# State space stage: half of the input projection in quarters between the scan's first pairs, phases and sine tables during the other half

## The chip, the core and the metric

The kernel runs on one core of a Trainium2 chip. A core has five engines with queues of their own: TensorE (PE in the profile, with its weight loads as PEld), VectorE (DVE), ScalarE (ACT), GpSimd (POOL) and SyncE (SP), which here only issues DMAs. They wait for one another by semaphores. The metric is the time of one execution in device microseconds (us), lower is better.

## The reference

Two networks follow one another. The first mixes with a gated delta rule and attention, then with a convolution; the second has three mixers in turn (an HGRN, an mLSTM, and a state space mixer, "S5"), each followed by a feed-forward stage, on 256 tokens of 1024 channels. Everything is computed in float32. The change touches only the last mixer:

```python
def _s5_mixer(x, w_in, a_re, a_im, log_dt, b_re, b_im, c_re, c_im, d_skip, w_out):
    u = (x @ w_in).astype(f32)
    dt = jnp.exp(log_dt.astype(f32))[:, None]
    mag = jnp.exp(a_re * dt)
    abar_re = mag * jnp.cos(a_im * dt)
    abar_im = mag * jnp.sin(a_im * dt)
    ...
    def step(carry, ub):
        hr, hi = carry
        bu_re = jnp.einsum('blgc,gpc->blgp', ub, bbar_re)
        bu_im = jnp.einsum('blgc,gpc->blgp', ub, bbar_im)
        pr, pi, sr, si = lax.associative_scan(_s5_combine, (a_r, a_i, bu_re, bu_im), axis=1)
        ...
        y = jnp.einsum('blgp,gcp->blgc', sr, c_re) - jnp.einsum('blgp,gcp->blgc', si, c_im)
        return (sr[:, -1], si[:, -1]), y
    ...
    y = y + d_skip.astype(f32) * u
    y = jax.nn.gelu(y).astype(x.dtype)
    za, zb = jnp.split(y @ w_out, 2, axis=-1)
    return za * jax.nn.sigmoid(zb)
```

`abar` is a complex number; a state is turned by its angle and shrunk by `mag` at every token.

## The kernel before

Activations lie with channels on the 128 partitions and the 256 tokens along the free axis (T = 256), in KC = 8 chunks. The program is a list of stages; each stage writes its part of every engine's queue, by hand and in program order, so the order of the code is the order of the queues. Weights come as slabs of 1 MB through a ring of five buffers that SyncE fills as they are freed. L216 is the helper that issues every matmul with weights. PSUM has eight banks: seven (BANKS) go round as jobs, and the eighth, `mod_bank`, is used by the first network's modulation.

The S5 mixer is two stages.

`S5In` projects the input: four slabs (`project_columns`), each two chunks of 128 channels and 16 products of 128x128 by 128x256, into a bank; ScalarE copies each bank to `u` (L3334). Beside it ScalarE and VectorE prepare coefficients in `columns`, 32 numbers a partition: `R_DT` (L3351, the angle in turns), `R_MAG` and `R_SIN` and `R_COS`, then with L3343 and a few others `R_CR` and `R_CI`; then VectorE scales the read-out matrices, loaded by DMA, in six operations over 1024 elements (L3379 to L3384) and two scalings (L3385, L3386). The last one raises `ready`.

`S5Scan` works through 32 tiles of 128 states, in 16 pairs. For a tile i:
- GpSimd makes the phase of every token (L3515 to L3517, three operations over 256 elements; two buffers, so tile i waits for the sines of tile i - 2). It waits for `ready` first.
- ScalarE makes a table of cosine and two sines (L3493 to L3499, five operations). There are six table buffers, so tile i waits until tile i - 6 has been turned back.
- TensorE projects the pair's input to states (L3468, `project`), VectorE multiplies it by the table (`turn`, L3527 and L3528), TensorE adds the terms up (L3450 and L3451, the "rotations"), VectorE scans in PSUM (`scan`, L3539 and L3540), multiplies by the table again (`turn_back`, L3550 and L3551), and TensorE reads out (L3482, `read_out`). Every fourth tile an output chunk is finished (L3573).

VectorE's order in pair m is scan(2m), scan(2m+1), turn(2m+2), turn(2m+3), perhaps a finish, turn_back(2m), turn_back(2m+1). TensorE's order in pair m is the rotations of 2m and 2m+1, the projection of pair m+1, the read-out of pair m-1. `project(m)` needs the copy of slab m // 4.

Of the kernel before, what the change touches and what calls it, by code (L numbers as in the profile page):

```python
# [21 lines left out]
P = 128  # L22
# [3277 lines left out]
class S5In(Stage):  # L3300


    def setup(self):
        k = self.k
        self.x_ready = k.h_ready
        self.slab0 = k.weights.reserve(4, False)
        self.u = k.area(S_U, KC, T)
        self.u_ready = k.counter("mixer_q").events(4)
        self.jobs = [k.job(e) for e in self.u_ready]
        self.loaded = k.counter("s5_matrices_loaded")  # L3310
        self.dt_ready = k.counter("s5_dt").event()
        self.prod_ready = k.counter("s5_products").events(2)
        self.exp_ready = k.counter("s5_exp").event()
        self.sin_ready = k.counter("s5_sin").event()
        self.ready = k.counter("decay_cumulated").event()

    def tensor(self, pe):
        project_columns(self.k, pe, (self.k.h,), self.x_ready, self.jobs)

    def scalar(self, act):  # L3320
        k, c = self.k, self.k.cols
        for e in self.x_ready:
            act.wait_ge(*e)
        act.dma_start(k.area(S_BC, 4096), k.s5_bc).then_inc(self.loaded.sem, 16)
        act.activation(c[:, R_DT, :], k.v("s5_log_dt", 0, S5_TILES), ACT.Exp).then_inc(self.dt_ready[0], 1)
        act.wait_ge(*self.prod_ready[0])
        act.activation(c[:, R_MAG, :], c[:, R_MAG, :], ACT.Exp).then_inc(self.exp_ready[0], 1)
        act.wait_ge(*self.prod_ready[1])

        act.activation(c[:, R_SIN, :], c[:, R_TH, :], ACT.Sin)  # L3330
        act.activation(c[:, R_COS, :], c[:, R_TH, :], ACT.Sin, scale=0.5).then_inc(self.sin_ready[0], 1)
        for j in range(4):
            act.wait_ge(*self.jobs[j].full)
            act.activation(self.u[:, 2 * j:2 * j + 2, :], pair(self.jobs[j]), ACT.Identity)\  # L3334
               .then_inc(self.u_ready[j][0], 1)

    def vector(self, dve):
        k, c, link = self.k, self.k.cols, self.k.dve.link
# [9 lines left out]
        tt(R_TH, aim, row(R_DT), mult)  # L3348
        reduce_angle(dve, link, row(R_TH), row(R_N), self.prod_ready[1])

        link(dve.tensor_scalar(row(R_DT), row(R_TH), 1.0 / TWO_PI, None, mult))  # L3351
        dve.wait_ge(*self.exp_ready)
        dve.wait_ge(*self.sin_ready)

# [18 lines left out]

        dve.wait_ge(self.loaded.sem, 16)
        out = k.area(S_BC + 2048, 2, S5_TILES, 32)
        t1, t2 = k.area(S_PH, S5_TILES, 32), k.area(S_T1, S5_TILES, 32)
        cr = row(R_CR).unsqueeze(2).broadcast_to([P, S5_TILES, 32])
        ci = row(R_CI).unsqueeze(2).broadcast_to([P, S5_TILES, 32])
        link(dve.tensor_tensor(t1, out[:, 0, :, :], ci, mult))  # L3379
# [20 lines left out]
class S5Scan(Stage):  # L3400
# [32 lines left out]
    def tensor(self, pe):  # L3433
        k = self.k
        b = k.area(S_BC, KC * 2, P)
        pe.wait_ge(self.src.loaded.sem, 16)
        pe.wait_ge(*self.src.ready)
        for bank in (*self.bu_banks, *self.g_banks, self.y_bank):
            begin(pe, bank)
        self.project(pe, b, 0)  # L3440
        for m in range(S5_PAIRS):
            for i in (2 * m, 2 * m + 1):
                bank = self.g_banks[i % 2].ap
                t1, t2 = self.turned[:, i % 2, 0:2, :], self.turned[:, i % 2, 2:4, :]
                pe.wait_ge(*self.turned_ready[i])
                if m >= 1:
                    pe.wait_ge(*self.scanned[i - 2])
                for part in range(2):
                    out = bank[:, part * T:(part + 1) * T]
                    pe.matmul(out, k.c("ident"), t1[:, part, :], start=True, stop=False)  # L3450
                    mm = pe.matmul(out, self.neg, t2[:, 1 - part, :], start=False, stop=True)  # L3451
                mm.then_inc(self.g_full[i][0], 1)
            if m + 1 < S5_PAIRS:
                self.project(pe, b, m + 1)
            if m >= 1:
                self.read_out(pe, m - 1)
        self.read_out(pe, S5_PAIRS - 1)
# [27 lines left out]

    def scalar(self, act):
        k = self.k
        for i in range(S5_TILES):
            table = self.table[:, i % S5_TABLES, :, :]
            act.wait_ge(*self.phase_ready[i])  # L3490
            if i >= S5_TABLES:
                act.wait_ge(*self.back_ready[i - S5_TABLES])
            act.activation(table[:, 1, :], self.phase[:, i % 2, 0, :], ACT.Sin, scale=TURN)  # L3493
            act.activation(table[:, 2, :], self.phase[:, i % 2, 0, :], ACT.Sin, scale=-TURN)
            act.activation(table[:, 0, :], self.phase[:, i % 2, 0, :], ACT.Sin, scale=0.5 * TURN)\
               .then_inc(self.sin_done[i][0], 1)
            act.wait_ge(*self.sin_done[i])
            k.act.link(act.activation(table[:, 0, :], table[:, 0, :], ACT.Square))
            act.activation(table[:, 0, :], table[:, 0, :], ACT.Identity, bias=k.eps[:, 2:3], scale=-2.0)\  # L3499
               .then_inc(self.table_ready[i][0], 1)  # L3500
# [4 lines left out]
    def gpsimd(self, pool):  # L3505

        k = self.k
        pool.wait_ge(*self.src.ready)
        for i in range(S5_TILES):
            if i >= 2:  # L3510

# [343 lines left out]
```

## Time and profile before

| | |
|---|---|
| three timed runs | 2686.16, 2687.28, 2688.93 us, median 2687.28 |
| the profiled execution | 2674.91 us, span 2673.1 us |
| busy in the span | PE 89%, PEld 80%, DVE 58%, ACT 40%, POOL 4% |
| input projection of S5, four slabs | 1802.18 to 1831.77 us |
| scan, first rotations to last read-out | 1835.84 to 1956.1 us |

The page gives busy shares for the whole span, the groups of instructions by line, and the chain of waits that ended last. The order of time gives for every piece its start, its length, the engine, the line, what it writes and reads, and in brackets how long the engine had been idle and who released it. The stage of the change is 154 us of the 2673, so the argument rests on its own stretch.

### The profile page before, as it was taken

How to read it: one execution, taken by the hardware profiler on the slowest of the kernel's cores; microseconds unless marked ns; L12 is line 12 of the kernel's file. 1: busy time of each engine (PE TensorE's matmuls, PEld its weight loads, DVE VectorE, ACT ScalarE, POOL GpSimd, SP SyncE). 2: the span in 40 equal slices, each digit the busy share in tenths (PEclk: the TensorE clock that was granted, in tenths of full speed). 3: DMA queues.
4: the chain of work that ended last, by engine and by line, in shares of the span. 5: the costliest groups of instructions: out<-in, count | busy, mean ns of one | idle time of the engine just before them, and what ended most of it. 6: DMA issues, size and time to landing. Idle time of an engine off the chain costs nothing.

```text
span 2673.1 us, 40276 instructions
## 1 busy us (share of the span) xinstructions
PE 2388.1 (89%) x17042; PEld 2151.2 (80%) x17042; DVE 1558.9 (58%) x2585; ACT 1067.4 (40%) x1682; POOL 111.3 (4%) x119
## 2 busy tenths in 40 slices
PE   6998998999889999589998879999998999757998
PEld 3665788998679989569997759997678998756998
DVE  3386456646846555556656446657946655664655
ACT  2424334443244345234444334434514335613443
POOL 0012000000000000000000000005600000000000
PEclk8999998999999999799998779999998999978999
DMA  7236353552135544014553115542034554301552
GB/s 294 111 142 259 136 181 135 189 190 79 64 142 187 187 158 164 14 48 176 189 188 111 64 47 190 190 158 79 1 111 163 186 188 152 117 1 49 203 190 80
DMA packets 50292, 368.27 MB, mean 138 GB/s; under 512 B 5568, under 2 KB 5696, under 8 KB 5824
## 3 DMA queue, kind: packets, MB, share of 16 engines
q1 hardware_dynamic: 49968, 363.59, 37.5%
q8 instruction: 135, 2.21, 0.3%
q10 hardware_dynamic: 144, 2.10, 0.2%
q14 instruction: 45, 0.37, 0.0%
HBM read 364.62 MB, written 1.05 MB: 137 GB/s over the span
## 4 chain that ended last, share of the span: by engine, by line
PE 79%; DVE 13%; ACT 5%; issue 2%; DMA 1%; SPq 0%; DVEq 0%; ACTq 0%
PE psum L216 63%; PE psum L2861 3%; DVE weight_parts L209 1%; PE psum L3450 1%; PE psum L3451 1%; DMA weight_ring<-stream_dram 1%; PE psum L2484 1%; PE psum L3187 1%; DVE work L949 1%; PE psum L398 1%; DVE work L2935 1%; DVE work L2936 1%; PE psum L1589 1%; PE psum L3468 1%; PE psum L543 1%
## 5 line engine op out<-in xcount | busy, mean ns | idle before, releaser
L216 PE MATMUL psum<-input_parts,weight_parts 128*128 128x256 f32 x8064 | 979.1, 284 | 57.0 <-DVE input_parts L957 27.3
L216 PEld LDWEIGHTS psum<-input_parts,weight_parts 128*128 128x128 f32 x8064 | 973.7, 192 | 64.8 <-issue 59.1
L209 DVE TENSOR_TENSOR weight_parts<-weight_ring,weight_parts 128x1024 fp32r<-128x1024 f32 x492 | 579.8, 1220 | 301.9 <-ACT weight_parts L193 300.9
L193 ACT ACTIVATE weight_parts<-weight_ring 128x1024 fp32r<-128x1024 f32 x492 | 492.9, 1052 | 198.1 <-PE psum L216 192.9
L216 PE MATMUL psum<-hidden_parts,weight_parts 128*128 128x256 f32 x3168 | 377.2, 281 | 0.0
L216 PE MATMUL psum<-work,weight_ring 128*128 128x256 f32 (+1 forms) x1376 | 354.7, 419 | 23.6 <-DVE work L2952 10.1
L216 PEld LDWEIGHTS psum<-hidden_parts,weight_parts 128*128 128x128 f32 x3168 | 374.6, 188 | 0.5
L216 PEld LDWEIGHTS psum<-work,weight_ring 128*128 128x128 f32 x1376 | 270.1, 198 | 103.6 <-issue 67.0
L1038 DVE TENSOR_TENSOR work<-work,psum 128x256 f32<-128x256 f32 x132 | 55.6, 421 | 287.3 <-ACT work L1031 287.3
L1031 ACT ACTIVATE work<-psum 128x256 f32<-128x256 f32 x132 | 50.8, 385 | 421.1 <-PE psum L216 421.0
L2861 PE MATMUL psum<-work 128*128 128x128 f32 x512 | 79.7, 331 | 56.7 <-DVE work L2936 56.7
L2861 PEld LDWEIGHTS psum<-work 128*128 128x128 f32 x512 | 77.4, 244 | 59.2 <-DVE work L2936 59.2
L216 PE MATMUL psum<-weight_parts,input_parts 128*128 128x256 f32 x576 | 75.3, 294 | 11.0 <-DVE weight_parts L209 11.0
L216 PEld LDWEIGHTS psum<-weight_parts,input_parts 128*128 128x128 f32 x576 | 74.0, 200 | 12.1 <-issue 12.1
L216 PE MATMUL psum<-weight_ring,silu_cond 128*32 128x256 f32 x768 | 54.4, 403 | 21.0 <-DMA weight_ring<-stream_dram 21.0
L2886 ACT ACTIVATE work<-work 128x2048 f32<-128x2048 f32 x16 | 30.3, 1908 | 96.3 <-DVE work L2925 96.3
L2527 DVE SCALAR_TENSOR_TENSOR work<-work,vectors 128x256 f32<-128x256 f32 x168 | 67.2, 477 | 0.0
L1042 DVE TENSOR_TENSOR hidden_parts<-work,hidden_parts 128x256 fp32r<-128x256 f32 x132 | 56.2, 425 | 4.5
L3515 POOL TENSOR_TENSOR work<-constants,columns 128x256 f32<-128x256 f32 x32 | 19.6, 612 | 868.6 <-DVE work L3386 840.7
L3450 PE MATMUL psum<-work,constants 128*128 128x256 f32 x128 | 40.7, 400 | 12.4 <-DVE work L3528 12.4
L216 PEld LDWEIGHTS psum<-weight_ring,silu_cond 128*32 128x32 f32 x768 | 20.8, 113 | 34.7 <-issue 16.6
L2905 POOL MEMSET work<- 128x3072 f32 x2 | 5.3, 2664 | 1014.7 <-DVE input_parts L709 722.6
(463 smaller groups left out, 2363.3 us busy)
## 6 DMA issues: line engine op xcount, KB each, us to landing
weight_ring<-stream_dram SPq DMA_DIRECT2D x341, 1024.0 KB, 4.8
constants<-constants_dram SPq DMA_DIRECT2D x1, 2176.0 KB, 15.3
work<-s_bc_dram ACTq DMA_DIRECT2D x1, 2048.0 KB, 8.0
work<-ctx_dram SPq DMA_DIRECT2D x1, 1024.0 KB, 7.2
residual<-x_dram SPq DMA_DIRECT2D x1, 1024.0 KB, 9.4
out_dram<-residual SPq DMA_DIRECT2D x1, 1024.0 KB, 3.9
vectors<-vectors_dram SPq DMA_DIRECT2D x1, 550.5 KB, 3.7
constants<-constants_dram SPq DMA_DIRECT2D x1, 65.0 KB, 3.5
```

The source lines that it names most:

```text
L193: act.activation(self.parts[:, s % SPLITS, 0, cols], self.ring[:, i % RING, cols], ACT.Identity)\
L209: ins = dve.tensor_tensor(self.parts[:, s % SPLITS, 1, cols], self.ring[:, i % RING, cols], self.parts[:, s % SPLITS, 0, cols].bitcast(F32 ...
L216: mm = pe.matmul(*args, **kw)
L398: return pe.matmul(mod_columns(k, layer, n, 1), rows, k.c("strip_sum"), start=True, stop=True)
L543: mm = pe.matmul(self.job.ap[:, 0:T], self.k.c("mean"), self.sq[:, c, :], start=(c == 0), stop=(c == KC - 1))
L1031: act.activation(self.hid[:, j % 2, :], job.ap[:, 0:T], ACT.Silu).then_inc(self.silu[j][0], 1)
L1038: dve.tensor_tensor(hid, hid, (job if j else self.up_job).ap[:, T:2 * T], ALU.mult).then_inc(self.whole[j][0], 1)
L1042: dve.tensor_tensor(lo, hid, hi.bitcast(F32), ALU.subtract).then_inc(self.ready[j][0], 1)
L2527: ins = dve.scalar_tensor_tensor(acc, src, w, acc, ALU.mult, ALU.add)
L2861: mm = pe.matmul(job.ap[:, i * P:(i + 1) * P], left[:, h, cols], right[:, h, cols], start=True, stop=True)
L2886: act.activation(self.e[:, l % 2, :], self.e[:, l % 2, :], ACT.Exp).then_inc(self.exp[l][0], 1)
L3450: pe.matmul(out, k.c("ident"), t1[:, part, :], start=True, stop=False)
```

## The change

The projection is cut in two. The first two slabs go as before. Of the third and fourth, a quarter (eight instructions in the trace: four products, each in two passes) is issued in each of the scan's pairs 0 to 7, between the projection of the next pair and the read-out (`project_part`). The three later jobs are no longer banks of the round but the spare `mod_bank`, one after the other, so job 2 waits for the copy of job 1, and job 3 for that of job 2.

ScalarE's four copies are taken out of `S5In.scalar` and put as `take` into the scan's queue: before table 0, and before tables 2, 8 and 16.

GpSimd's first phase waits for `prod_ready[2]`, which VectorE raises with `R_DT`, and not for `ready`. Since phases are then written while VectorE still prepares, the preparation's scratch (`t1`) moves out of the phases' place.

```diff
@@ S5In.setup
-        self.jobs = [k.job(e) for e in self.u_ready]
+        self.jobs = [k.job(self.u_ready[0])]
+        full = k.bank_full[0].events(3)
+        for n in range(1, 4):
+            before = self.u_ready[n - 1] if n >= 2 else None
+            self.jobs.append(Job(k.mod_bank, before, full[n - 1], self.u_ready[n]))
...
-        self.prod_ready = k.counter("s5_products").events(2)
+        self.prod_ready = k.counter("s5_products").events(3)
...
     def tensor(self, pe):
-        project_columns(self.k, pe, (self.k.h,), self.x_ready, self.jobs)
+        project_columns(self.k, pe, (self.k.h,), self.x_ready, self.jobs[0:2])
+
+    def project_part(self, pe, j, part):
+
+        k, job, half = self.k, self.jobs[j], part // 2
+        if part == 0:
+            begin(pe, job)
+            self.slab = k.weights.next(pe)[0].rearrange("p (k c) -> p k c", k=KC)
+        for c in range(4 * (part % 2), 4 * (part % 2) + 4):
+            mm = k.weights.matmul(pe, job.ap[:, half * T:(half + 1) * T], self.slab[:, c, half * P:(half + 1) * P],
+                                  k.h[:, c, :], start=(c == 0), stop=(c == KC - 1))
+        if part == 3:
+            mm.then_inc(job.full[0], 1)
+
+    def take(self, act, j):
+
+        act.wait_ge(*self.jobs[j].full)
+        act.activation(self.u[:, 2 * j:2 * j + 2, :], pair(self.jobs[j]), ACT.Identity)\
+           .then_inc(self.u_ready[j][0], 1)
@@ S5In.scalar
-        for j in range(4):
-            act.wait_ge(*self.jobs[j].full)
-            act.activation(self.u[:, 2 * j:2 * j + 2, :], pair(self.jobs[j]), ACT.Identity)\
-               .then_inc(self.u_ready[j][0], 1)
@@ S5In.vector
-        link(dve.tensor_scalar(row(R_DT), row(R_TH), 1.0 / TWO_PI, None, mult))
+        dve.tensor_scalar(row(R_DT), row(R_TH), 1.0 / TWO_PI, None, mult).then_inc(self.prod_ready[2][0], 1)
...
-        t1, t2 = k.area(S_PH, S5_TILES, 32), k.area(S_T1, S5_TILES, 32)
+        t1, t2 = (k.area(S_T1 + i * 1024, S5_TILES, 32) for i in range(2))
@@ S5Scan.tensor
             if m + 1 < S5_PAIRS:
                 self.project(pe, b, m + 1)
+            if m < 8:
+                self.src.project_part(pe, 2 + m // 4, m % 4)
             if m >= 1:
                 self.read_out(pe, m - 1)
@@ S5Scan.scalar
+        self.src.take(act, 0)
         for i in range(S5_TILES):
+            if i in (2, 8, 16):
+                self.src.take(act, 1 + i // 8)
@@ S5Scan.gpsimd
-        pool.wait_ge(*self.src.ready)
+        pool.wait_ge(*self.src.prod_ready[2])
```

On GpSimd, at the start of the scan, the first phase of before stands behind VectorE's last scaling (`decay_cumulated` is `ready`):

```order
L3515 TENSOR_TENSOR work<-constants,columns 128x256 [waits decay_cumulated]
L3516 TENSOR_SCALAR work<-work 128x256 [waits pool_chain]
L3517 TENSOR_TENSOR work<-work 128x256 [waits pool_chain]
L3515 TENSOR_TENSOR work<-constants,columns 128x256
L3516 TENSOR_SCALAR work<-work 128x256 [waits pool_chain]
L3517 TENSOR_TENSOR work<-work 128x256 [waits pool_chain]
L3515 TENSOR_TENSOR work<-constants,columns 128x256 [waits pair_exp]
```

and now behind its products (`pair_exp` counts the sines that ScalarE has made):

```order
L3538 TENSOR_TENSOR work<-constants,columns 128x256 [waits s5_products]
L3539 TENSOR_SCALAR work<-work 128x256 [waits pool_chain]
L3540 TENSOR_TENSOR work<-work 128x256 [waits pool_chain]
L3538 TENSOR_TENSOR work<-constants,columns 128x256
L3539 TENSOR_SCALAR work<-work 128x256 [waits pool_chain]
L3540 TENSOR_TENSOR work<-work 128x256 [waits pool_chain]
L3538 TENSOR_TENSOR work<-constants,columns 128x256 [waits pair_exp]
```

The operations are the same; the first one's wait has moved ahead of all that VectorE does after the products.

On TensorE, one pair of the scan (pair 3) before (`s5_turned` is VectorE's first multiplication, `s5_turned_back` its last):

```order
L3450 MATMUL psum<-work,constants 128x256 [waits s5_scanned,s5_turned]
L3451 MATMUL psum<-work 128x256
L3450 MATMUL psum<-work,constants 128x256
L3451 MATMUL psum<-work 128x256
L3468 MATMUL psum<-work 128x256 [waits mixer_q,s5_turned]
L3468 MATMUL psum<-work 128x256 x3
L3482 MATMUL psum<-work 32x256 [waits s5_turned_back]
L3482 MATMUL psum<-work 32x256 x7
```

and now:

```order
L3468 MATMUL psum<-work,constants 128x256 [waits s5_scanned,s5_turned]
L3469 MATMUL psum<-work 128x256
L3468 MATMUL psum<-work,constants 128x256
L3469 MATMUL psum<-work 128x256
L3488 MATMUL psum<-work 128x256 [waits mixer_q,s5_turned]
L3488 MATMUL psum<-work 128x256 x3
L216 MATMUL psum<-residual,weight_ring 128x256 x4
L3502 MATMUL psum<-work 32x256 [waits s5_turned_back]
L3502 MATMUL psum<-work 32x256 x7
```

Four products of a slab stand between the projection and the read-out; the rest has only new line numbers.

On ScalarE, between the tables of tiles 7 and 8, before:

```order
L3498 ACTIVATE work<-work 128x256 [waits pair_exp]
L3499 ACTIVATE work<-work,epsilons 128x256 [waits act_chain]
L3493 ACTIVATE work<-work 128x256 [waits s5_turned_back,s5_phase]
L3494 ACTIVATE work<-work 128x256
L3495 ACTIVATE work<-work 128x256
```

and now:

```order
L3521 ACTIVATE work<-work 128x256 [waits pair_exp]
L3522 ACTIVATE work<-work,epsilons 128x256 [waits act_chain]
L3339 ACTIVATE work<-psum 128x512 [waits bank0_full]
L3516 ACTIVATE work<-work 128x256 [waits s5_turned_back,s5_phase]
L3517 ACTIVATE work<-work 128x256
L3518 ACTIVATE work<-work 128x256
```

The copy of the third slab (L3339) stands in the queue between the two tables and waits for that slab's last quarter.

## Rows read from the trace of the kernel before

**Rows 1.** The page: the chain of waits, share of the span by engine.
```profile
PE 79%; DVE 13%; ACT 5%; issue 2%; DMA 1%; SPq 0%; DVEq 0%; ACTq 0%
```

**Rows 2.** Order of time, projection to round 1: start us, us, engine line op [idle before].
```profile
1802.18 29.55 PE L216 MATMUL psum<-residual,weight_ring 128*128 128x256 f32 x128 [3.03 <-ACT residual L865]
...
1808.82 0.18 DVE L3351 TENSOR_SCALAR columns<-columns 128x32 f32<-128x32 f32 x1
...
1809.41 0.19 DVE L3343 TENSOR_TENSOR columns<-columns 128x32 f32<-128x32 f32 x1 [0.41 <-ACT columns L3331]
...
1811.05 0.60 ACT L3334 ACTIVATE work<-psum 128x512 f32<-128x512 f32 x1 [1.78 <-PE psum L216]
...
1814.42 1.23 DVE L3379 TENSOR_TENSOR work<-work,columns 128x1024 f32<-128x1024 f32 x1 [1.06 <-DMA work<-s_bc_dram]
...
1817.96 0.60 ACT L3334 ACTIVATE work<-psum 128x512 f32<-128x512 f32 x1 [6.31 <-PE psum L216]
...
1822.11 0.69 DVE L3386 TENSOR_SCALAR work<-work 128x1024 f32<-128x1024 f32 x1
1822.88 0.61 POOL L3515 TENSOR_TENSOR work<-constants,columns 128x256 f32<-128x256 f32 x1 [840.74 <-DVE work L3386]
...
1825.42 0.62 POOL L3515 TENSOR_TENSOR work<-constants,columns 128x256 f32<-128x256 f32 x1
...
1831.77 0.60 ACT L3334 ACTIVATE work<-psum 128x512 f32<-128x512 f32 x1 [6.31 <-PE psum L216]
1832.27 0.41 ACT L3493 ACTIVATE work<-work 128x256 f32<-128x256 f32 x1
...
1832.62 1.13 PE L3468 MATMUL psum<-work 32*128 32x256 f32 x8 [0.88 <-ACT work L3334]
...
1833.76 0.51 ACT L3499 ACTIVATE work<-work,epsilons 128x256 f32<-128x256 f32 x1
...
1834.50 0.69 DVE L3527 TENSOR_TENSOR work<-psum,work 128x512 f32<-128x512 f32 x1 [11.70 <-ACT work L3499]
...
1835.84 0.70 PE L3450 MATMUL psum<-work,constants 128*128 128x256 f32 x2 [2.09 <-DVE work L3528]
...
1843.79 0.70 PE L3450 MATMUL psum<-work,constants 128*128 128x256 f32 x2 [1.48 <-DVE work L3528]
```

**Rows 3.** Busy time by stretch: us; PE, PEld, DVE, ACT, POOL; granted clock; DMA.
```profile
1836.00:1838.00 2.00, 2.00 (x7) 1.65 (x8) 1.29 (x2) 1.94 (x6) 1.83 (x3) 0.67 0.00 0
1838.00:1840.00 2.00, 2.00 (x6) 1.55 (x6) 1.13 (x2) 1.53 (x5) 1.91 (x3) 0.50 0.00 0
```

**Rows 4.** Order of time, one steady round of the scan on TensorE.
```profile
1865.48 0.70 PE L3450 MATMUL psum<-work,constants 128*128 128x256 f32 x2 [0.86 <-DVE work L3528]
...
1869.13 1.13 PE L3468 MATMUL psum<-work 32*128 32x256 f32 x8
...
1870.19 1.92 PE L3482 MATMUL psum<-work 128*32 128x256 f32 x16
...
1872.58 0.70 PE L3450 MATMUL psum<-work,constants 128*128 128x256 f32 x2 [0.47 <-DVE work L3528]
```

**Rows 5.** The chain of waits in order of time: where round 8 begins.
```profile
1894.66 0.70 PE psum L3450 x2
```

**Rows 6.** VectorE beside GpSimd elsewhere: two lines' durations (min/median/max), then order of time.
```profile
L1491 DVE SCALAR_TENSOR_TENSOR work<-work,vectors x48: 483/752/1452, 50.4 to 187.2; 128x512 f32<-128x512 f32 x32, 128x256 f32<-128x256 f32 x16
...
L1637 DVE TENSOR_SCALAR work<-work,columns x16: 485/486/2241, 204.5 to 286.9; 128x512 f32<-128x512 f32 x16
...
162.36 1.03 POOL L1913 COPY spare<-spare 32x1024 f32<-32x1024 f32 x1 [118.41 <-ACT spare L1812]
...
162.48 1.45 DVE L1491 SCALAR_TENSOR_TENSOR work<-work,vectors 128x512 f32<-128x512 f32 x1
163.44 1.39 POOL L1913 COPY spare<-spare 32x1024 f32<-32x1024 f32 x1
...
248.88 1.92 POOL L1913 COPY work<-spare 32x1024 f32<-32x1024 f32 x1
249.03 2.06 DVE L1637 TENSOR_SCALAR work<-work,columns 128x512 f32<-128x512 f32 x1
```

## The prediction

> **What bounds the kernel now.** I read the profile in four views: the chain of waits for the whole program, the order of time over the start of the state space stage, the same view over one steady pair of the scan, and the places where VectorE and GpSimd run side by side. The chain lies 79% on TensorE [rows 1], but the average says little about this stage, so it has to be read from its own rows.
>
> The stage has two parts. In the first TensorE multiplies four slabs from 1802.18 to 1831.77; ScalarE copies the results out at 1811.05, 1817.96 and so on to 1831.77, so a slab at full clock is 6.91 us [rows 2]. Beside it VectorE prepares the coefficients: narrow operations on 32 elements from 1809.41, a wait of 1.06 us for the matrices' transfer, then six wide ones on 1024 elements and two scalings, done at 1822.80 (1822.11 and 0.69) [rows 2]. GpSimd, which makes the phases, waits for that whole preparation and starts at 1822.88 [rows 2]. So in the first part the projection is late (1831.77), and the preparation has 9 us to spare.
>
> Then comes the scan: I call the time from TensorE's first rotation matmul of one pair to that of the next a round. Round 0 starts at 1835.84, after the last copy (1831.77), the first table (1832.27 to 1834.27), and VectorE's two multiplications (1834.50 to 1835.84) [rows 2]. A steady round lasts 7.10 us (1865.48 to 1872.58), or 7.49 in every other one, in which an output chunk is finished. In it TensorE works until 1870.19 + 1.92 = 1872.11 and is idle 0.47 us; VectorE is the engine it waits for [rows 4]. So both are nearly full: TensorE has only 0.5 to 0.9 us a round to give away. Eight rounds, 0 to 7, take 1835.84 to 1894.66, 58.8 us [rows 2, 5].
>
> **Part 1: two slabs leave the front.** The projection ends at 1817.96 instead of 1831.77, 13.8 us earlier [rows 2]. It is no longer last; VectorE's preparation is, at 1822.80 if nothing disturbs it. The most that the front can give is thus the way from there: the first projection matmuls (1.13 us, 1832.62) and VectorE's 1.34, so round 0 would start at about 1825.5, 10.3 us earlier.
>
> **Part 2: GpSimd starts 14 us earlier, beside VectorE's preparation.** The tables and phases themselves now lie under the projection and cost nothing. But before, GpSimd and the preparation never overlapped: one started when the other was through. Elsewhere in the program they do overlap. A VectorE operation on 512 elements with two inputs in SBUF takes 0.75 us at the median, and 1.45 us while GpSimd copies; GpSimd's copy goes from 1.03 to 1.39 us at the same place. A one-input scaling goes from 0.49 to 2.06 us [rows 6]. They take turns, one instruction of each. In the scan they run side by side with no such effect, and there each VectorE multiplication takes one input from PSUM. The preparation's operations have all their inputs in SBUF, so I take them to behave as [rows 6].
>
> The narrow operations after 1809.41 are 14 products and sums, 2 scalings and a reciprocal. Each waits for the one before it, so each of the 16 would let one GpSimd operation in between. GpSimd's three operations for a phase take 2.54 us (1822.88 to 1825.42), 0.85 each [rows 2]. 16 x 0.85 = 13.6, so the narrow part ends at 1823.0 instead of waiting for the transfer until 1814.42: +8.6 us. For the wide ones I take the difference of [rows 6]: +0.70 us against a copy of 1.03, that is the GpSimd operation less 0.33; with GpSimd's mean of about 0.80 that is 0.47 for each of 8 operations, +3.8 us. Together +12.4: the preparation ends at 1835.2. GpSimd has enough work for this: it makes eight phases (24 operations, as many as 16 + 8) before it needs a table buffer that the scan must free. The bounds: 0 if GpSimd loses every turn (sharing can't make VectorE quicker); 24 x 0.80 = 19 us, less the 1.06 of the transfer, if VectorE waits out each operation in full.
>
> The Trainium skill ("SBUF — State Buffer", section "Who interferes with whom") says that a VectorE instruction with two SBUF inputs contends with a GpSimd one that reads SBUF, and that the loser blocks for the whole instruction. The first half agrees with [rows 6]; by the second each wide operation would lose 0.80 and not 0.47, which would add 2.6 us to the sum.
>
> **Part 3: the start of the scan.** TensorE has then been idle since 1817.96, so I price its next work at the low level. The profile shows the granted clock at 0.67 and 0.50 of full just after the last such gap, at 1836 to 1840 [rows 3]. The first projection matmuls thus take 2.2 us instead of 1.13. 1835.2 + 2.2 + 1.34 = 1838.8, +3.0 us against 1835.84.
>
> **Part 4: eight rounds with a quarter of a slab each.** A quarter is 6.91 / 4 = 1.73 us, placed between the projection of the next pair and the read-out. TensorE's own work in a round is 1872.11 - 1865.48 = 6.63, or 6.4 without the 0.27 that the first matmul after a wait takes longer [rows 4]; with the quarter, 8.17. That is over VectorE's 7.10 to 7.49, so TensorE becomes the bound of these rounds. Round 0 has no read-out, but the low clock: 9.0 (it was 7.95, 1835.84 to 1843.79 [rows 2]). Rounds 1, 2, 5, 6: 4 x 8.17 = 32.7.
>
> Rounds 3 and 7 have a new wait. ScalarE's copy of the projected slab stands just ahead of table 8 (and 16) on its queue, and needs the fourth quarter, which TensorE runs in round 3 (7) only after that round's rotations. Table 8 is what VectorE needs for the next pair in the same round. The way from the round's start is 3.46 (rotations) + 1.09 (projection) + 1.73 (quarter), then the copy 0.60, the table 2.0, VectorE's 1.34: 10.2, with 0.1 for the signals 10.3. Only the read-out lies beside it. TensorE then sits idle for 2 us. Table 9 comes 2.0 later again, which makes round 4 about 8.4. Queued behind ScalarE's wait are only tables; the ones already made were used up by then. So 9.0 + 32.7 + 8.4 + 2 x 10.3 = 70.7 against 58.8: +11.9 us. Round 8 still settles, +0.5. From round 9 on all is as before, as is the next stage: the weight ring is refilled long before the scan ends.
>
> **The sum.** 3.0 + 11.9 + 0.5 = +15.4 us. The profiled execution was 2674.91 us (span 2673.1, 1.8 around it), so it would become 2690.3. The three timed runs had a median of 2687.28, 12.4 above the profiled one; I add the same +15.4 there: 2702.7 us, +0.57%.
>
> **The rivals.**
> *Only the wide operations are disturbed* (narrow ones slip between GpSimd's). For: no row shows a 32-element operation beside GpSimd. Then the preparation ends at 1822.8 + 3.8 = 1826.6, round 0 starts at 1830.1, 5.7 early, and the rounds cost the same 12.4: +6.7, 2694.0.
> *No contention.* Against: [rows 6]. Round 0 starts at 1822.80 + 2.2 + 1.34 = 1826.3 with the clock low, 9.5 early, and the rounds take 12.4 more: +2.9, 2690.2; from 0 to +4 with the clock, 2687 to 2691. This is "no change": the 10 us won at the front go back in the rounds.
> *Faster.* One mechanism: no contention, and the copy ahead of table 8 doesn't hold VectorE, because tables run further ahead than I read. Then no round is over 8.17: 8 x 8.17 = 65.4, +6.5, against a start 10.3 to 12 us earlier at full clock: -4 to -6, 2682. It decides at the point where the eight rounds cost less than the earlier start. For it: ScalarE is under half busy in the scan. Against: the table buffers free only two tables a round.
> *VectorE waits out everything*, and the 2 us gaps in rounds 3 and 7 bring the low clock back for some rotations: prelude +18, gaps +2: +22, 2709.
>
> **How the numbers follow.** Forecast 0.50 (its own range 2699 to 2706), wide only 0.17, no contention 0.17, faster 0.07, everything waits 0.09. 0.2% is 5.4 us, about what a measurement of this kernel can tell from no change. Faster 0.07; within 0.2% (no contention, and 0.03 of "wide only") 0.20; slower 0.73. The range 2688 to 2709 takes in all but the faster case and edges.
>
> **What would show it.** In the profile after: VectorE's narrow operations at 0.8 to 1.1 us instead of 0.19, the wide ones at 1.5 to 1.9 instead of 1.22; the last scaling ending near 1835 instead of 1822.80; TensorE idle from 1818 until then; rounds of 8.2 with two of 10.3, in which ScalarE waits for the quarter and TensorE for VectorE. If the wide operations still take 1.22, part 2 is wrong. If the rounds with a quarter stay at 7.1 to 7.5, TensorE had more room than I read. If round 3 is no longer than round 2, the copy's place is harmless.

## The result, and the profile after

The changed kernel takes 2694.05 us (median of 12), the kernel before 2687.78 (median of 12): a ratio of 1.0023, 95% interval 1.0012 to 1.0033, so 6.3 us slower (3.2 to 8.9). The forecast was slower by 15.4 us. The sign held and the range held the time; the size was more than twice too large, because one term of the sum was wrong in sign.

The stage of the change lies 9.8 us later in this execution than in the profiled one of before, for reasons ahead of it, so I count from the start of the projection's first matmul (1811.95 here, 1802.18 in [rows 2]) to the first matmul of the next stage. That was 153.9 us before (to 1956.07) and is 161.4 now (1811.95 to 1973.38): 7.5 more, which agrees with the 6.3 of the timed runs within their interval.

The page of the kernel after, its chain of waits by engine, against [rows 1]; as there, it says little about this stage:

```profile
PE 80%; DVE 11%; ACT 5%; issue 2%; DMA 1%; SPq 0%; DVEq 0%; ACTq 0%
```

The order of time of the kernel after, from the projection to the first rotations; it answers [rows 2]. L3361 is the narrow product of before's L3343, L3397 the first wide operation, L3404 the last scaling, L3538 to L3540 GpSimd's phase, L3488 the pair's projection, L3468 the rotation.

```profile
1811.95 15.74 PE L216 MATMUL psum<-residual,weight_ring 128*128 128x256 f32 x64 [3.03 <-ACT residual L865]
...
1819.14 0.35 DVE L3361 TENSOR_TENSOR columns<-columns 128x32 f32<-128x32 f32 x1 [0.39 <-ACT columns L3353]
1819.53 0.18 DVE L3374 TENSOR_SCALAR columns<-columns 128x32 f32<-128x32 f32 x1
1819.53 1.10 POOL L3539 TENSOR_SCALAR work<-work 128x256 f32<-128x256 f32 x1
...
1820.26 0.19 DVE L3361 TENSOR_TENSOR columns<-columns 128x32 f32<-128x32 f32 x1
...
1820.72 0.77 POOL L3540 TENSOR_TENSOR work<-work 128x256 f32<-128x256 f32 x1
...
1820.93 0.61 DVE L3361 TENSOR_TENSOR columns<-columns 128x32 f32<-128x32 f32 x1
...
1824.74 1.23 DVE L3397 TENSOR_TENSOR work<-work,columns 128x1024 f32<-128x1024 f32 x1
1824.74 2.15 POOL L3539 TENSOR_SCALAR work<-work 128x256 f32<-128x256 f32 x1
...
1826.98 0.91 POOL L3540 TENSOR_TENSOR work<-work 128x256 f32<-128x256 f32 x1
1827.33 1.63 DVE L3399 TENSOR_TENSOR work<-work,columns 128x1024 f32<-128x1024 f32 x1
...
1833.99 0.68 DVE L3404 TENSOR_SCALAR work<-work 128x1024 f32<-128x1024 f32 x1
...
1834.77 2.08 PE L3488 MATMUL psum<-work 32*128 32x256 f32 x8 [7.08 <-issue]
...
1838.33 1.22 PE L3468 MATMUL psum<-work,constants 128*128 128x256 f32 x2 [1.48 <-DVE work L3551]
```

Read it from below. The first rotations come 26.4 us after the projection's start; it was 33.7. The preparation ends at 1834.67, 22.7 us after it; it was 20.6. TensorE has been idle for 7 us and does the small projection at the low clock, 2.08 us instead of 1.13. The narrow operations are hardly touched: beside the rounding (L3539) those shown keep their 0.18 and 0.19 us (the worst in this trace takes 0.40), and one that meets a product (L3540) waits for its end, 0.61. The first wide operation takes 1.23, as alone, and it is GpSimd's rounding beside it that takes 2.15 instead of 1.07.

Then the rounds. Two stretches of the kernel after, a whole round each, rounds 2 and 3 (columns as in [rows 3]):

```profile
1855.74:1864.23 8.49, 8.49 (x51) 5.92 (x49) 6.88 (x12) 0.00 (x0) 0.00 (x0) 1.00 0.00 0
1864.23:1874.85 10.62, 8.56 (x51) 5.92 (x49) 6.50 (x11) 3.77 (x10) 2.12 (x3) 1.00 0.01 2
```

In round 2 TensorE is busy for all of 8.49 us: it is the bound. In round 3 it does the same 8.56 and sits idle for 2.06. The waits over the scan, kernel after: who waited for whom, us in total, times, the longest:

```profile
ACT work L3339 <- PE psum L216: 34.9, 2, 17.5
...
DVE work L3550 <- ACT work L3522: 9.1, 4, 3.9
...
PE psum L3468 <- DVE work L3551: 9.3, 9, 2.1
```

They are the three links of the new wait: ScalarE's copy waits 17.5 us twice for a slab's last quarter, VectorE 3.9 us for the table behind it, TensorE 2.1 us for VectorE.

### The profile page after: what moved, and what is told of

It is laid out like the page before. It is cut to its first block, busy times and chain, and to the rows that moved or that the text cites. A ratio compares the mean times of both kernels' runs of the same rounds, so it can differ in the third digit from the quotient of the medians.

```text
span 2693.3 us, 40275 instructions
## 1 busy us (share of the span) xinstructions
PE 2405.0 (89%) x17042; PEld 2163.9 (80%) x17042; DVE 1561.7 (58%) x2585; ACT 1067.6 (40%) x1682; POOL 116.3 (4%) x119
## 3 DMA queue, kind: packets, MB, share of 16 engines
HBM read 364.62 MB, written 1.05 MB: 136 GB/s over the span
## 4 chain that ended last, share of the span: by engine, by line
PE 80%; DVE 11%; ACT 5%; issue 2%; DMA 1%; SPq 0%; DVEq 0%; ACTq 0%
PE psum L216 64%; PE psum L2861 3%; DVE weight_parts L209 1%; PE psum L3468 1%; PE psum L3469 1%; DMA weight_ring<-stream_dram 1%; PE psum L2484 1%; PE psum L3187 1%; PE psum L3488 1%; DVE work L949 1%; PE psum L398 1%; PE psum L543 1%; DVE work L2935 1%; DVE work L2936 1%; PE psum L1589 1%
## 5 line engine op out<-in xcount | busy, mean ns | idle before, releaser
L216 PE MATMUL psum<-work,weight_ring 128*128 128x256 f32 (+1 forms) x1376 | 354.8, 419 | 23.5 <-DVE work L2952 10.1
L216 PEld LDWEIGHTS psum<-weight_parts,input_parts 128*128 128x128 f32 x576 | 72.6, 196 | 13.6 <-issue 13.6
L3538 POOL TENSOR_TENSOR work<-constants,columns 128x256 f32<-128x256 f32 x32 | 21.5, 673 | 878.1 <-DVE columns L3369 833.4
L3468 PE MATMUL psum<-work,constants 128*128 128x256 f32 x128 | 42.1, 412 | 9.3 <-DVE work L3551 9.3
## 6 DMA issues: line engine op xcount, KB each, us to landing
residual<-x_dram SPq DMA_DIRECT2D x1, 1024.0 KB, 10.2
```

The lines of the kernel that those rows point to most:

```text
L216: mm = pe.matmul(*args, **kw)
```

## Experiments

Nine more kernels, in the order in which they ran. Six were timed in 8 to 12 executions; the three that add an operation to GpSimd's queue were executed once each, and only their traces are read. Stages and rounds come from one profiled execution of each kernel. Where I give a place, it is counted from the projection's first matmul, and "the stage" is from there to the next stage's first matmul; it was 153.9 us before and 161.4 in the changed kernel.

**The copies ahead of tables 8 and 16.** The changed kernel with

```diff
-            if i in (2, 8, 16):
+            if i in (2, 12, 20):
                 self.src.take(act, 1 + i // 8)
```

> The changed kernel, but ScalarE's copies of the third and fourth slab stand before tables 12 and 20 instead of 8 and 16. Theory A (TensorE is the bound of the eight rounds, and the early place of the copies costs about 2.1 us of TensorE idle in rounds 3 and 7): both rounds go from 10.6 to 8.5 us, the stage gets 4.4 us shorter than in the changed kernel, ratio to the kernel before about 1.0008. Rival B (the long rounds come from something else that the copy only happens to wait for): rounds 3 and 7 stay over 10 us, ratio 1.0023 as for the changed kernel.

Measured: ratio 1.0010 to the kernel before (0.9998 to 1.0023). Rounds 3, 4, 7 and 8, with no idle time on TensorE left:

```profile
1863.48:1871.96 8.48, 8.48 (x50) 5.93 (x48) 8.36 (x15) 4.40 (x11) 4.78 (x6) 1.00 0.01 2
1871.96:1880.45 8.49, 8.49 (x50) 5.93 (x48) 6.52 (x11) 3.79 (x10) 4.78 (x6) 1.00 0.25 76
...
1897.43:1905.92 8.49, 8.49 (x51) 5.93 (x49) 8.37 (x15) 4.39 (x11) 4.78 (x6) 1.00 0.00 0
1905.92:1912.48 6.56, 6.56 (x42) 4.49 (x40) 5.67 (x10) 3.80 (x10) 4.61 (x6) 1.00 0.01 2
```

Rounds 0 to 7 together take 67.7 us instead of 72.8, and round 8 is 6.56 instead of 8.25. So the wait was the copy's place, as theory A had it. It cost 4.4 us in rounds 3, 4 and 7 (the other 0.6 of the 5.1 is round 0, 8.39 instead of 9.03, with the granted clock at 0.78 instead of 0.72, ahead of either copy), and a further 1.7 in round 8. That last part neither theory had: after the second gap the granted clock is low for a while, which the row of round 8 in the changed kernel shows (0.79 granted):

```profile
1911.11:1919.36 8.25, 8.25 (x40) 5.66 (x40) 7.66 (x13) 6.57 (x17) 7.74 (x11) 0.79 0.01 2
```

It is the same 8.25 at 0.79 in all five kernels that keep the copies' place (the changed one and four of those below), and in none does the first gap, in round 3, lower it (round 4 is 8.67 at 1.00). The stage is 156.2 us, 5.3 less than in the changed kernel and still 2.3 more than before; at its end this execution has 1.5 us of low clock in the last read-outs (10.5 to 12.1 us) that is not of the change. The timed runs can't tell this kernel from the changed one (1.0010 and 1.0023, with intervals that overlap); what the place costs is read from the traces.

**GpSimd late again.** The changed kernel with

```diff
-        pool.wait_ge(*self.src.prod_ready[2])
+        pool.wait_ge(*self.src.ready)
```

> The changed kernel, but GpSimd again waits for the end of VectorE's preparation, so the two never overlap before the scan. Theory A (the turns that VectorE loses to GpSimd cost 2.1 us, and the early tables give as much back): the preparation ends 20.6 us after the projection's start instead of 22.7, but the first table then is late (2.6 us of phase, 2.0 of table), and the first rotations come 26.5 us after the projection's start, against 26.4 in the changed kernel; ratio to the kernel before 1.0023. Rival B (contention costs more than it shows, also in the scan): at least 2 us faster than the changed kernel, ratio 1.0015 or less.

Measured: 1.0029 (1.0014 to 1.0043), the changed kernel's 1.0023 within the interval. The preparation ends at 20.5 (expected 20.6), the first rotations come at 26.8 (26.5): GpSimd's first phase, the table, and then VectorE stand in a row where the contention stood. The order of time:

```profile
1827.41 0.69 DVE L3404 TENSOR_SCALAR work<-work 128x1024 f32<-128x1024 f32 x1
...
1828.18 0.61 POOL L3538 TENSOR_TENSOR work<-constants,columns 128x256 f32<-128x256 f32 x1 [845.52 <-DVE work L3404]
...
1830.78 0.42 ACT L3516 ACTIVATE work<-work 128x256 f32<-128x256 f32 x1 [13.73 <-POOL work L3540]
...
1833.03 0.69 DVE L3550 TENSOR_TENSOR work<-psum,work 128x512 f32<-128x512 f32 x1 [4.93 <-ACT work L3522]
...
1834.37 1.22 PE L3468 MATMUL psum<-work,constants 128*128 128x256 f32 x2 [4.44 <-DVE work L3551]
```

So the second half of the change, the early phases and tables, is worth 0.4 us at this place (26.8 against 26.4): it saves the 4.6 us of phase and table, and loses 2.2 to contention (22.7 against 20.5) and the rest because the first small projection, which needs 2.1 at the low clock, was running meanwhile anyway.

**The tables alone.** The kernel before, all four slabs in front, with GpSimd's early start, the scratch moved, and the copies between the tables:

```diff
-        for j in range(4):
-            act.wait_ge(*self.jobs[j].full)
-            ...
+        self.src.take(act, 0)
+            if i in (2, 4, 6):
+                self.src.take(act, i // 2)
-        pool.wait_ge(*self.src.ready)
+        pool.wait_ge(*self.src.prod_ready[2])
```

> The kernel before, with all four slabs in front, and only the other half of the change: GpSimd starts right after the angles, ScalarE's copies stand between the first tables. Theory A (contention stretches the preparation by 2 us, which here lies under the projection): the preparation ends at 22.7 us after the projection's start, the first rotations come at 32.3 instead of 33.7, rounds stay at 7.1 and 7.5: 1.4 us faster than before, ratio 0.9995. Rival B (the overlap of GpSimd and VectorE costs more than early tables give): no faster or slower, ratio 1.000 or more.

Measured: 1.0006 (0.9994 to 1.0018), no difference that can be told. In the trace the preparation ends at 22.7, as expected, and hidden. The first rotations come at 34.2, not 32.3. Two things make the first rotations late: the low clock at the projection's start lasted longer in this execution (granted 0.67 over the first 8.85 us, where it is 0.81 in the changed kernel's), which makes four slabs 30.75 us instead of 29.6; and TensorE still waits 0.89 us for the fourth slab's copy. Round 0 in return is 6.27 instead of 7.95, at full clock; why the clock stayed up isn't shown, since TensorE had waited 1.48 us just ahead of it, and after 1.49 us the clock was low in the next two kernels. The stage is 152.8 us, 1.1 less than before, but all of that is round 0: the start itself came 0.6 later, behind slabs that ended 1.2 later. Theory A's gain of 1.4 at the start can't be read from this, and the interval holds both its 0.9995 and rival B's 1.000 or more, so this run decides nothing.

**One slab instead of two.** Three slabs in front, the fourth in rounds 0 to 7, two products in each; the third slab goes to a bank of the round, and `project_part` now takes the first and last product:

```diff
-        project_columns(self.k, pe, (self.k.h,), self.x_ready, self.jobs[0:2])
+        project_columns(self.k, pe, (self.k.h,), self.x_ready, self.jobs[0:3])
...
+S5_PARTS = (0, 2, 4, 6, 8, 10, 12, 14, 16)
-            if m < 8:
-                self.src.project_part(pe, 2 + m // 4, m % 4)
+            if m < len(S5_PARTS) - 1:
+                self.src.project_part(pe, S5_PARTS[m], S5_PARTS[m + 1])
-            if i in (2, 8, 16):
-                self.src.take(act, 1 + i // 8)
+            if i in (2, 5, 20):
+                self.src.take(act, 1 + (2, 5, 20).index(i))
```

> Three slabs in front; only the fourth goes into the scan, two products (of 16) in each of rounds 0 to 7; its copy stands before table 20, the third's before table 5. GpSimd early. Theory A (the front is bound by the preparation at 22.7 us, which three slabs of 6.9 reach as well, and a round has room for 0.5 to 0.9 us on TensorE): first rotations at 25.3 us after the projection's start, 8.3 us before those of the kernel before; rounds 7.7 us, 8 of them 61.6 plus 1 for a low clock against 58.8; in sum 5 us faster than before, ratio 0.998. Rival B (whatever is put into the rounds costs its whole time there, and each visit 0.2 more): 8.3 gained and 8.5 given back, ratio 1.000.

Measured: 0.9972 (0.9959 to 0.9986), faster than both kernels. The preparation ends at 22.7 as before, the first rotations come at 26.4 and not 25.3 (the low clock in the first slab again lasted long, so that the slabs ended at 23.8). Rounds 1 to 7 are 7.63 each, against 7.7 expected:

```profile
1856.08:1863.71 7.63, 7.63 (x47) 5.16 (x45) 7.59 (x15) 3.80 (x10) 4.78 (x7) 1.00 0.00 0
```

Rounds 0 to 7 take 61.3 us where they took 58.8 before, so 7.3 us won at the front cost 2.5 in the rounds. Rival B (8.5 given back) is out. The start is the same as in the changed kernel, by two ways of like length: here the slabs end at 23.8 and the small projection takes 1.13 at full clock, there the preparation ends at 22.7 and it takes 2.08 at the low one. So taking the third slab out of the front had bought nothing.

**One slab over eleven rounds.** As the last one, with one product in even rounds and two in odd ones:

```diff
-S5_PARTS = (0, 2, 4, 6, 8, 10, 12, 14, 16)
+S5_PARTS = (0, 1, 3, 4, 6, 7, 9, 10, 12, 13, 15, 16)
-            if i in (2, 5, 20):
-                self.src.take(act, 1 + (2, 5, 20).index(i))
+            if i in (2, 5, 26):
+                self.src.take(act, 1 + (2, 5, 26).index(i))
```

> As the run with one slab in the scan, but its 16 products go over rounds 0 to 10, one in even rounds and two in odd ones, and its copy stands before table 26. Theory A (a round's length is the larger of VectorE's 7.1 or 7.5 and TensorE's 6.56 + 0.43 a product + 0.2 a visit, so one product is 7.2 and two 7.6): rounds 0 to 10 average 7.4, the stage is 1 us shorter than with two products in eight rounds (7.63 each), ratio to the kernel before 0.997. Rival B (each visit costs on its own, whatever room there is): three visits more cost 0.6, ratio 0.998 or more.

Measured: 0.9964 (0.9950 to 0.9978). Rounds of one and of two products:

```profile
1851.55:1858.74 7.19, 7.19 (x44) 4.78 (x43) 7.19 (x14) 3.80 (x10) 4.88 (x7) 1.00 0.01 2
1858.74:1866.37 7.63, 7.63 (x47) 5.17 (x45) 7.63 (x14) 3.80 (x10) 4.93 (x7) 1.00 0.00 0
```

The stage is 148.4 us, 1.2 less than with two products in eight rounds, 1 expected; the whole program can't tell these two apart. With round 8 of the first experiment, where there is no product and TensorE never waits, there are four cases: 6.56 with none, 7.19 with one, 7.63 with two, 8.49 with four. Those with products lie on one line, 0.43 a product, which would give 6.76 for none: a visit costs 0.2 us on top.

**Which of GpSimd's operations holds VectorE.** The forecast took turns for all of them. Two kernels double one operation of GpSimd's phase for tiles 0 to 5:

```diff
             k.pool.link(pool.tensor_tensor(x, k.c("time"), turns, ALU.mult))
+            if i < 6:
+                k.pool.link(pool.tensor_tensor(x, k.c("time"), turns, ALU.mult))
```

> The changed kernel, with GpSimd's first operation of a phase (a product of two inputs, 0.61 us) issued twice for tiles 0 to 5; the second one writes the same values. Theory A (a narrow operation of VectorE waits only for GpSimd's operations with two SBUF inputs, to their end, and hardly for its rounding): VectorE's narrow part from the first product after the sines to the first wide operation, 5.6 us in the changed kernel, gets longer, 6.0 to 6.8. Rival B (they take turns instruction by instruction whatever GpSimd runs): doubling changes little, since the narrow part would already have waited 16 times; it would have been 13.6 us. Rival C (the delays are of the rounding): no longer, 5.6 or less.

Measured: the narrow part takes 5.4 us (1828.35 to 1833.78), not 6.0 to 6.8; the wide part 10.1 us, in the changed kernel 9.9. A miss for theory A, which had it longer than the changed kernel's 5.6, and for rival B, whose 13.6 is far off. The number is the one that rival C named (5.6 or less, the delays being of the rounding), but the rows speak against C: GpSimd's doubled product holds the narrow product beside it to its end, while a scaling with one input passes it, and the next narrow product passes the rounding:

```profile
1828.73 0.66 POOL L3540 TENSOR_TENSOR work<-constants,columns 128x256 f32<-128x256 f32 x1
1828.74 0.18 DVE L3374 TENSOR_SCALAR columns<-columns 128x32 f32<-128x32 f32 x1
1828.95 0.48 DVE L3361 TENSOR_TENSOR columns<-columns 128x32 f32<-128x32 f32 x1
...
1829.48 1.10 POOL L3541 TENSOR_SCALAR work<-work 128x256 f32<-128x256 f32 x1
1829.69 0.27 DVE L3361 TENSOR_TENSOR columns<-columns 128x32 f32<-128x32 f32 x1
```

Five of GpSimd's products run beside the narrow part in either kernel. Here each holds one narrow product, and only for as long as it still runs; in the changed kernel four do, and the fifth meets the reciprocal, which has one input and keeps its 0.35. Together the holds come to 1.3 us in either kernel: more of them, and each shorter.

```diff
             k.pool.link(pool.tensor_scalar(n, x, ROUND, ROUND, ALU.add, ALU.subtract))
+            if i < 6:
+                k.pool.link(pool.tensor_scalar(n, x, ROUND, ROUND, ALU.add, ALU.subtract))
```

> The changed kernel, with GpSimd's second operation of a phase (the rounding, one SBUF input, 1.07 us) issued twice for tiles 0 to 5; the second one writes the same values. Theory A (the rounding hardly holds VectorE): the narrow part gets shorter or stays, 4.8 to 5.6 us, since fewer of GpSimd's two-input operations fall into it, and the eight wide and scaling operations take less than 9.9 us, about 9.3. Rival B (turns whatever GpSimd runs) or C (the rounding is what delays): both parts at least as long as in the changed kernel, 5.6 and 9.9, or longer.

Measured: the narrow part takes 5.2 us (1823.55 to 1828.70), within 4.8 to 5.6; the wide part 10.2 and not 9.3, of which 0.44 is the last scaling, caught by a GpSimd product (1.12 instead of 0.68). The order of time while two roundings run one behind the other:

```profile
1823.96 1.10 POOL L3539 TENSOR_SCALAR work<-work 128x256 f32<-128x256 f32 x1
1824.17 0.27 DVE L3361 TENSOR_TENSOR columns<-columns 128x32 f32<-128x32 f32 x1
1824.47 0.18 DVE L3377 TENSOR_SCALAR columns<-columns 128x32 f32<-128x32 f32 x1
1824.69 0.19 DVE L3361 TENSOR_TENSOR columns<-columns 128x32 f32<-128x32 f32 x1
1824.91 0.42 DVE L3361 TENSOR_TENSOR columns<-vectors 128x32 f32<-128x32 f32 x2
1825.14 1.11 POOL L3541 TENSOR_SCALAR work<-work 128x256 f32<-128x256 f32 x1
1825.36 0.27 DVE L3361 TENSOR_TENSOR columns<-columns 128x32 f32<-128x32 f32 x1
```

The six narrow operations shown, five of them with two inputs, pass in 2.3 us of rounding, and the worst of them loses 0.08. Rivals B and C had the narrow part no shorter than 5.6, so they are out there; the longer wide part is as they had it.

**Two phases early, the rest late.** As with eleven rounds, but GpSimd waits for the end of the preparation before phase 2, and the third slab's copy stands before table 3 instead of 5:

```diff
-            if i in (2, 5, 26):
-                self.src.take(act, 1 + (2, 5, 26).index(i))
+            if i in (2, 3, 26):
+                self.src.take(act, 1 + (2, 3, 26).index(i))
...
+            if i == 2:
+                pool.wait_ge(*self.src.ready)
             if i >= 2:
                 pool.wait_ge(*self.sin_done[i - 2])
```

> As the run with one slab over eleven rounds, but GpSimd makes only phases 0 and 1 early and waits for the end of the preparation before phase 2; the third slab's copy stands before table 3. Theory A (what GpSimd does beside the wide operations costs 1.5 us at the start, and the first two tables are all that the start needs): the preparation ends 20.9 us after the projection's start instead of 22.7, so the slabs (22.7, or 24 if the low clock lasts longer) set the start, TensorE has no gap, first rotations at 25.3 instead of 26.4; ratio to the kernel before 0.996. Rival B (the later phases then come too late for pairs 1 and 2): the rounds 0 and 1 get longer by as much as the start gains or more, ratio as with the phases early.

Measured: 0.9974 (0.9961 to 0.9988), neither better nor worse than with the phases early (0.9964). The preparation ends at 20.8 (20.9 expected), so the contention with the wide operations is gone; the first rotations come at 26.35 and not 25.3, because the slabs ended late in this execution. In the kernel with eleven rounds they ended just as late (23.8), so the slabs set both starts, and what the contention costs at the start is not tested here. Round 0 is 6.26 instead of 7.88, at full clock. The stage is 145.5 us, the shortest of all, but its 2.9 us of difference are clock alone: 1.6 in round 0 and 1.3 in the last round, with all others equal. The timed runs confirm none of it. Nor is the gap ahead of round 0 the difference, for it is the same 1.49 us. First the kernel with eleven rounds, where the first rotation begins a round at 0.79, then this one, at 1.00:

```profile
1836.04 1.22 PE L3470 MATMUL psum<-work,constants 128*128 128x256 f32 x2 [1.49 <-DVE work L3553]
...
1833.73 0.70 PE L3470 MATMUL psum<-work,constants 128*128 128x256 f32 x2 [1.49 <-DVE work L3555]
```

Rival B's late phases didn't show: round 1 is 7.63 in both.

**A copy on GpSimd.** [Rows 6] show copies, and copies are what the forecast was sized by. The changed kernel with

```diff
             k.pool.link(pool.tensor_tensor(x, k.c("time"), turns, ALU.mult))
+            if i < 2:
+                k.pool.link(pool.tensor_copy(k.area(S_P, 1024), k.const[:, 0:1024]))
```

> The changed kernel, with a copy of 1024 elements a partition (one SBUF input, into space that nobody uses then) added to GpSimd's queue behind the first operation of phases 0 and 1, so that two copies run beside VectorE's narrow operations. It tells why a copy held VectorE elsewhere and the rounding, also of one input, does not here. Theory A (it depends on the operation and not on the number of inputs: a copy keeps VectorE's two-input operations waiting to its end, as elsewhere in this program, the rounding does not): a narrow operation that falls into a copy takes 0.4 to 1.0 us, and the narrow part gets 0.5 to 2 us longer than the 5.6 of the changed kernel. Rival B (GpSimd's one-input operations do not hold narrow operations at all, only wide ones meet them): narrow operations keep 0.2 to 0.3 us during the copies, the narrow part stays at 5.6 or less.

Measured: the narrow part takes 6.4 us (1817.76 to 1824.18), 0.8 more. The order of time:

```profile
1818.14 1.04 POOL L3540 COPY work<-constants 128x1024 f32<-128x1024 f32 x1
1818.16 1.05 DVE L3374 TENSOR_SCALAR columns<-columns 128x32 f32<-128x32 f32 x1
...
1821.86 1.04 POOL L3540 COPY work<-constants 128x1024 f32<-128x1024 f32 x1
1821.88 1.29 DVE L3361 TENSOR_TENSOR columns<-columns 128x32 f32<-128x32 f32 x2
1822.98 1.12 POOL L3541 TENSOR_SCALAR work<-work 128x256 f32<-128x256 f32 x1
```

A scaling of 32 elements takes 1.05 us beside the copy, to its very end, and 0.18 elsewhere; two products take 1.29 beside the second copy, and 0.42 elsewhere. That is theory A: a copy holds VectorE as in [rows 6], a rounding, also of one SBUF input and just as long, does not. The run doesn't separate the operation from the amount, though: in the same time the copy moves 1024 elements and the rounding 256. A copy of 256 elements, or a rounding of 1024, was not run.

## Why the prediction was wrong

By its own steps:

- *Part 1, the front is bound by the preparation:* right. The two slabs end 15.7 us after the projection's start, 13.8 earlier than the four, and the start then waits for the preparation.
- *Part 2, turns between VectorE and GpSimd, +12.4 us:* this is the step that failed. Measured +2.1 (20.6 to 22.7). The narrow operations were to wait 16 times, once for each; they grew from 3.9 to 5.6 us, and 1.06 of that growth was hidden, since the narrow part had waited as long for the transfer before. The error was to carry rows of a copy over to a rounding and to products of another length. The rounding is 1.07 of a phase's 2.4 us, and beside it up to five narrow operations pass, so GpSimd had only its products to hold VectorE with, each once and for what was left of it. Of the wide ones I had +3.8; it was +1.6 (9.9 against 8.4), since beside a rounding a wide operation takes 1.30 and beside a product 1.52 to 1.63, and GpSimd's operations took most of the waiting (2.15, 1.59 and 1.92 instead of 1.07, 0.61 and 1.07). The bound of 0 "if GpSimd loses every turn" was the nearer one. I had put it in the range, and given the case only 0.17.
- By the rule of the Trainium skill ("SBUF — State Buffer", section "Who interferes with whom": the loser blocks for the whole instruction) the term would have been an estimated 2.6 us larger still. The copy run agrees with it (1.05 us beside a copy of 1.04); the rounding does not: narrow operations with two SBUF inputs pass beside it in 0.19 to 0.40 us. Here the measurement decides.
- *Part 3, the small projection at the low clock, 2.2 us:* right, 2.08. The start of the scan was thus 7.3 us early and not 3.0 late. The forecast's own case of no contention had 9.5 early, 2.1 of which the real contention took.
- *Part 4, TensorE becomes the bound:* right, with the terms a little small. The eight rounds took 72.8 us, forecast 70.7, before 58.8. A quarter costs 1.93 and not 1.73: products put between matmuls of another shape cost 0.2 a visit, which the rounds of 0, 1, 2 and 4 products show. And the round without a product is 6.56 us, where I had 6.4: the way from rotation to projection is 3.65 us in round 2, where TensorE waits for nobody, the same as in [rows 4], so the 0.27 that I took off was mostly not there to take. (6.4 and 1.73 are also 8.13 and not 8.17.)
- *The copy ahead of table 8:* right in place and size, 10.6 against 10.3 for a round, idle 2.06 against 2, round 4 8.67 against 8.4. Round 8 was to settle at +0.5 and took +1.15, by the low clock after the second gap; the forecast had that only in its slowest rival. For the rival "faster" it said that ScalarE is under half busy in the scan; in rounds 0 to 7 of the kernel before it is busy 34.7 of 58.8 us, 59%.
- *The sum:* -7.3 + 14.0 + 1.1, less 0.3 in round 9, is 7.5 in the stage, 6.3 (3.2 to 8.9) in the timed runs. The rival "only the wide operations are disturbed" named +6.7 with about this picture; it was right in total partly by luck, for two errors nearly cancel: it had the start 5.7 early where it was 7.3, and the rounds at 12.4 where they were 14.8.

What the change was worth is thus: 7.3 us at the front, all of it and 7.5 more given back in the rounds. Most of that was avoidable: 6.1 us by the place of two copies (4.4 of waiting and 1.7 of clock), and the rest because it took two slabs out where one was enough. What stays open is why the rounding doesn't hold VectorE and the copy does; the runs tell that it is so, and not whether the kind of operation or its fewer elements in the same time make the difference. And one wait was left as it was: TensorE's first small projection stands behind `ready` in the code, though the matrices that it reads are not among those that VectorE scales. It takes 2.08 us behind the preparation in the changed kernel; no run tried it earlier.

## What to carry to other kernels

Before work is moved from a front into a loop, read two numbers: what bounds the front once the work is gone, and how much room the loop has on that engine in each round. Here the front had room for one slab and the loop for 0.5 to 0.9 us a round, and a version that takes just that is 0.36% faster (0.22 to 0.50) where twice as much was 0.23% slower. A wait put into an in-order queue belongs as late as its own reader allows, not where its data might first be ready: moving two copies by four places in ScalarE's queue took 6.1 us out of the rounds in the traces; the timed runs can't tell the two kernels apart.

## What the runs showed of the hardware

- GpSimd's rounding of 256 elements (one SBUF input, two scalars, 1.07 us) lets VectorE's narrow operations with two SBUF inputs pass (0.19 to 0.27 us each, one 0.40, against 0.19 alone), a copy of 1024 elements of the same length (1.04 us) holds them to its end (1.05 us, a scaling with one input too), and a product of two inputs (0.61 and 0.73 us) holds at most one two-input operation, to its own end, while one-input ones pass (a scaling in 0.18, the reciprocal in 0.35). Wide VectorE operations in turn stretch all of GpSimd's: a rounding from 1.07 to 2.15 us, a product from 0.61 to 1.59.
- A gap of 2.06 us on TensorE lowered the granted clock in one place (after round 7, 0.79 over the next 8.25 us) and not in another (after round 3, 1.00), the same in five kernels. And a gap of 1.48 or 1.49 us ahead of round 0 was followed by a low clock in two executions (0.79 over the round: one slab in eight and in eleven rounds) and by full clock in two (tables alone, two phases early). The length of the gap alone doesn't tell which.
- A group of products put between matmuls of other shapes costs TensorE 0.2 us a visit beside 0.43 a product.
